# A hybrid recurrent step with expert retrieval: the loading of the tokens, the turning of the caches and the first retrieval groups in another order

## What is computed

```python
def layer(h, states, p, lead):
    mix, new = token_mixer(rmsnorm(h, p['ln1']), conv_buf, s_dn, shift_buf, s_rw, p, lead)
    h = h + mix
    f = peer_ffn(rmsnorm(h, p['ln2']).reshape(B * T, D), p['peer_wq'], p['peer_keys'], p['peer_u'], p['peer_v'])
    return h + f, new                      # then rmsnorm with ln_f

def peer_ffn(x, wq, keys, u_tab, v_tab):   # for every token t, head h: 16 of 16384 experts
    q = (xb @ wq).reshape(PEER_BLOCK, PEER_HEADS, 2, PEER_HALF)
    s = jnp.einsum('thpc,hpnc->thpn', q, keys)
    sv, si = lax.top_k(s, K)               # K = 16, in each half
    ...                                    # 16 best sums of the two halves, their expert numbers eidx
    gates = jax.nn.softmax(cv.astype(jnp.float32), -1)
    h = jax.nn.gelu(jnp.einsum('thkd,td->thk', u_tab[eidx], xb).astype(jnp.float32))
    return jnp.einsum('thk,thkd->td', (gates * h).astype(xb.dtype), v_tab[eidx])
```

## Time and profile before

| | us |
|---|---|
| median of three runs (1186.66 to 1190.22) | 1186.82 |
| the profiled execution | 1191.67 |
| its span, as the trace shows it | 1189.9 |
| PE busy in the span | 1003.9 |
| DVE busy | 712.4 |
| POOL busy (issuing gathers) | 518.2 |
| ACT busy | 271.3 |
| bytes moved by gathers, at 59% of 16 engines' span | 276.86 MB |

### The profile page before, as it was taken

One profiled execution on the slowest core, in us unless ns is written; L12 is line 12 of the kernel. 1 busy time (PEld: TensorE's weight loads), 2 busy tenths in 40 slices (PEclk: granted clock), 3 DMA queues, 4 the chain that ended last, 5 costly groups with the idle time before them and its releaser, 6 DMA issues.

```text
span 1189.9 us, 11394 instructions
## 1 busy us (share of the span) xinstructions
PE 1003.9 (84%) x3771; PEld 572.1 (48%) x3771; DVE 712.4 (60%) x1879; ACT 271.3 (23%) x644; POOL 518.2 (44%) x595
## 2 busy tenths in 40 slices
PE   4999898999998998979798777777777777777788
PEld 3887666879997653855343222222222222222221
DVE  1014673895264627696477657756766775676653
ACT  2127464014233011211112111111122111111111
POOL 3000010000000002575766777777777777777763
PEclk9999899998997999889899999999999999999999
DMA  8152020443216434989999999999999999999997
GB/s 278 38 211 77 0 73 11 100 130 112 72 72 226 145 104 145 405 340 360 403 390 371 403 410 409 410 409 409 409 409 409 409 409 410 408 408 409 391 374 279
DMA packets 119784, 334.26 MB, mean 281 GB/s; under 512 B 19087, under 2 KB 33266, under 8 KB 119462
## 3 DMA queue, kind: packets, MB, share of 16 engines
q0 software_dynamic: 76032, 276.86, 59.0%
q1 hardware_dynamic: 43694, 56.68, 14.8%
HBM read 326.99 MB, written 5.74 MB: 280 GB/s over the span
## 4 chain that ended last, share of the span: by engine, by line
PE 39%; DMA 25%; DVE 18%; POOL 10%; issue 5%; ACT 2%; SPq 1%; DVEq 0%; ACTq 0%; POOLq 0%
PE bank L1395 36%; DMA sb_all<-in_peer_u,idx 14%; DMA sb_all<-in_peer_v,idx 10%; POOL sb_all L585 10%; DVE sb_all L1120 3%; ACT sb_all L1791 2%; DVE sb_all L1098 1%; DVE sb_all L1096 1%; DVE sb_all L1100 1%; DVE sb_all L2274 1%; DVE sb_all L2271 1%; DMA sb_all<-in_w_in 1%; DVE key_i L1068 1%; DVE sb_all L1061 1%; DVE key_i L1062 1%
## 5 line engine op out<-in xcount | busy, mean ns | idle before, releaser
L1395 PE MATMUL bank<-sb_all 128*128 128x512 f32 (+15 forms) x3462 | 968.6, 433 | 150.7 <-DMA sb_all<-in_peer_v,idx 138.1
L1395 PEld LDWEIGHTS bank<-sb_all 128*128 128x128 f32 (+7 forms) x3462 | 540.8, 187 | 573.6 <-DMA sb_all<-in_peer_v,idx 311.6
L1120 DVE CUSTOM_DVE_ANT_0 sb_all<-sb_all,bank 128x1024 f32<-128x1024 f32 x264 | 314.2, 1220 | 173.3 <-DMA sb_all<-in_peer_u,idx 172.8
L585 POOL DMA_INDIRECT sb_all<-in_peer_u,idx x264 | 251.5, 953 | 229.7 <-DVE idx L1104 103.3
L585 POOL DMA_INDIRECT sb_all<-in_peer_v,idx x264 | 250.9, 950 | 84.9 <-issue 68.6
L1791 ACT ACTIVATE sb_all<-sb_all 128x128 f32<-128x128 f32 (+11 forms) x367 | 145.1, 421 | 532.7 <-PE bank L1395 382.3
L1791 ACT ACTIVATE sb_all<-bank 128x264 f32<-128x264 f32 (+15 forms) x183 | 82.9, 468 | 362.8 <-PE bank L1395 312.1
L620 POOL IOTA sb_all<- 128x54 f32 x1 | 0.2, 183 | 166.5 <-PE bank L1395 166.5
L1385 POOL MEMSET sb_all<- 128x3456 f32 x1 | 3.0, 2984 | 142.8 <-DVE sb_all L2185 142.8
L2068 DVE SCALAR_TENSOR_TENSOR sb_all<-sb_all 128x288 f32<-128x288 f32 x14 | 6.1, 513 | 60.7 <-ACT sb_all L1791 60.7
L1791 ACT ACT_TABLE_LOAD x23 | 29.5, 1283 | 13.8 <-POOL sb_all L1364 9.5
(11 more groups left out here) (230 smaller groups left out, 435.1 us busy)
## 6 DMA issues: line engine op xcount, KB each, us to landing
sb_all<-in_w_in SPq DMA_DIRECT2D x9, 2048.0 KB, 7.7
sb_all<-in_peer_wq SPq DMA_DIRECT2D x4, 2048.0 KB, 16.0
sb_all<-in_w_in SPq DMA_DIRECT2D x5, 1024.0 KB, 5.2
sb_all<-in_peer_u,idx POOLq DMA_INDIRECT x264, 10.3
sb_all<-in_peer_v,idx POOLq DMA_INDIRECT x264, 10.4
out<-sb_all SPq DMA_DIRECT2D x8, 512.0 KB, 4.8
sb_all<-in_w_out SPq DMA_DIRECT2D x2, 2048.0 KB, 8.3
sb_all<-in_x_prompt SPq DMA_DIRECT2D x4, 512.0 KB
```

What stands on the lines that cost most here:

```text
L585: pool.indirect_dma_start(ring[at % 8], None, table[0], bass.IndirectOffsetOnAxis(ap=idx[:, c:c + 1], axis=0)).then_inc(landed[at % 8], 16)
L1120: v.tensor_tensor_reduce(uring[i % 8], uring[i % 8], x, 1.0, 0.0, ALU.mult, ALU.add, hdot[:, u % 2, j:j + 1]).then_inc(u_free, 1)
L1395: return nc.tensor.matmul(out, lhsT, rhs, start=start, stop=stop, **kw)
```

## The change

Beginning: six of the parameter loads are issued by ACT's own queue, the other five stay on SP; the caches and the six small loads go behind the weights `r`. POOL makes `ident` and the first `eps` column first and counts `consts` for them, then the other constants (the table `level` has only its two used planes filled). ACT takes a root of `eps` first, then for each tile, when it has landed, the square and the root. The caches are turned on PE between the projections of `r` and `kr`, and copied out by ACT after the first four output tiles.

Retrieval: on DVE the rest of the residual and the norms of tiles 1 and 2 come before any dot, then eight dots of unit 0, the second selection, the other eight. On ACT the Tanh of unit 0 comes before the copy of the fourth query tile, the softmax exponent of unit 1 behind the scores, and the Tanh of units 1, 2 and 3 at slots 8, 8 and 10 in place of 12. On POOL four v rows are gathered behind u row 15.

```diff
@@ retrieval, POOL: pool_peer
+            AHEAD = 4
             for i in range(NSLOT + LAG):
...
                     gather(pool, uring, u_in, peer_u, i, i)
-                if i >= LAG:
+                if i == PT - 1:
+                    for n in range(AHEAD):
+                        gather(pool, vring, v_in, peer_v, V_ORDER[n], n)
+                if i >= LAG + AHEAD:
@@ retrieval, ACT: act_rest
             softmax_exp(0)
-            softmax_exp(1)
             queried(0, slice(128, NX), 4, lambda q: psv(2 + q % 2, 128, NX - 128))
             scored(0, 1)
             scored(0, 2)
-            for q in range(4):
+            for q in range(3):
                 queried_all(1, q)
             gelu(0)
+            queried_all(1, 3)
             pair_scored(1)
+            softmax_exp(1)
+            GELU_AT = {0: 8, 1: 8, 2: 10}
...
-                    if j == 12 and u + 1 < UNITS:
+                    if j == GELU_AT.get(u, 12) and u + 1 < UNITS:
                         gelu(u + 1)
@@ retrieval, DVE: vec_rest
             topk(0)
             residual(3)
-            topk(1)
-            norm(1, 128)
             residual(4)
             residual(5)
-            dots(0, 0, 2)
+            norm(1, 128)
             norm(2, NS)
-            dots(0, 2, PT)
+            dots(0, 0, PT // 2)
+            topk(1)
+            dots(0, PT // 2, PT)
             weights(0)
@@ beginning, SP
-            for name, n in PAR:
+            emit_parameters(sp, PAR[6:])
...
-            sp.dma_start(cconv[0:24, :], cache_dn_conv[0].rearrange("b j n -> (b j) n")).then_inc(small_in, 16)
-            sp.dma_start(cshift[0:8, :], cache_rw_shift[0, :, 0]).then_inc(small_in, 16)
...
                 sp.dma_start(dst, src).then_inc(w_landed[slot], 16)
                 if n == 0:
+                    sp.dma_start(cconv[0:24, :], cache_dn_conv[0].rearrange("b j n -> (b j) n")).then_inc(small_in, 16)
+                    sp.dma_start(cshift[0:8, :], cache_rw_shift[0, :, 0]).then_inc(small_in, 16)
                     sp.dma_start(lora[0:64, :], rw_w2[0]).then_inc(small_in, 16)
@@ beginning, POOL
+            step(nc.gpsimd.memset(ident, 0.0))
+            step(nc.gpsimd.memset(eps[:, 0:1], 1e-6))
+            step.sync()
+            nc.gpsimd.affine_select(out=ident, in_=ident, pattern=[[-1, 128]], compare_op=ALU.not_equal, fill=1.0,
+                                    base=0, channel_multiplier=1).then_inc(consts, 1)
...
-            for l in range(LEVELS + 1):
+            for l in (LEVELS - 1, LEVELS):
@@ beginning, PE
-                    pe.wait_ge(small_in, 16 * 8)
...
             pe.wait_ge(xT_done, 8)
-            for name in ("r", "kr", "vr", "wag"):
+            pe.wait_ge(consts, 2)
+            project("r")
+            pe.wait_ge(small_in, 16 * 8)
+            for f in range(12):
+                nc.tensor.transpose(psv(7, 128, 24, at=24 * f), cconv[0:24, f * 128:(f + 1) * 128],
+                                    ident[0:24, 0:24])
...
+            for name in ("kr", "vr", "wag"):
                 project(name)
@@ beginning, ACT
-            act.wait_ge(x_in, 64)
+            emit_parameters(act, PAR[:6])
             act.wait_ge(consts, 1)
+            step(fn(eps[:, 3:4], eps[:, 0:1], ACT.Sqrt))
             for i, n in enumerate(TILE_ROWS):
+                act.wait_ge(x_in[i].sem, x_in[i].at(16 if i < 2 else 32))
                 step(fn(xs[0:n, i, :], xtok[0:n, i, :], ACT.Square, accum_out=ss[0:n, i:i + 1]))
-            for i, n in enumerate(TILE_ROWS):
-                step.sync(2 - i)
+                step.sync()
                 fn(rs[0:n, i:i + 1], ss[0:n, i:i + 1], ACT.Sqrt, scale=1.0 / D,
                    bias=eps[0:n, 0:1]).then_inc(rs_ready, 1)
```

More of the change, by code:

```diff
@@ L259, in hybrid_step @@
         w_landed = [sem(f"w_landed{i}") for i in range(3)]
-        x_in = sem("x_in")
+        x0_in = Signal(sem("x0_in"), 0)
+        x1_in, rows_in = series(sem("x1_rows_in"), 16, 32)
+        x2_in, keys_in = series(sem("x2_keys_in"), 32, 16)
+        x_in = [x0_in, x1_in, x2_in]
         small_in = sem("small_in")
@@ L1234, in hybrid_step, with emit_parameters @@
         block = ctx.enter_context(nc.Block())
-        @block.sync
-        def _(sp):
-            sp.dma_start(xtok[:, 0, :], x_prompt[0, 0:128]).then_inc(x_in, 16)
-            sp.dma_start(xtok[:, 1, :], x_prompt[0, 128:256]).then_inc(x_in, 16)
-            sp.dma_start(xtok[0:NS, 2, :], x_sample[:, 0]).then_inc(x_in, 16)
-            sp.dma_start(xtok[NS:NS + META, 2, :], meta_tokens).then_inc(x_in, 16)
+        def emit_parameters(eng, rows):
             srcs = {"ln1": ln1, "mu": rw_mu, "w0": rw_w0, "a0": rw_a0, "k_k": rw_k_k, "k_a": rw_k_a, "gn_w": rw_gn_w,
                     "gn_b": rw_gn_b, "dn_norm": dn_norm_w}
-            for name, n in PAR:
+            for name, n in rows:
                 if name == "conv":
@@ L1251, in _ @@
                     src = srcs[name][0].rearrange("(f p) -> f p", p=128)
[L1252 to L1254 removed]
+                eng.dma_start(parrow[PAR_AT[name]:PAR_AT[name] + n, :], src).then_inc(par_in, 16)
+        @block.sync
+        def _(sp):
+            sp.dma_start(xtok[:, 0, :], x_prompt[0, 0:128]).then_inc(x0_in.sem, 16)
+            sp.dma_start(xtok[:, 1, :], x_prompt[0, 128:256]).then_inc(x1_in.sem, 16)
+            sp.dma_start(xtok[0:NS, 2, :], x_sample[:, 0]).then_inc(x2_in.sem, 16)
+            sp.dma_start(xtok[NS:NS + META, 2, :], meta_tokens).then_inc(x2_in.sem, 16)
+            emit_parameters(sp, PAR[6:])
             for n, (name, src, slot, width, use) in enumerate(items):
@@ L1322, in _ @@
             step = Steps(pool, pool_step)
-            for t, v in ((ones, 1.0), (ident, 0.0), (halves, 0.0), (incl, 1.0), (strict, 1.0),
-                         (level, 0.0), (reset, 1.0), (ba, 0.0), (prw[:, :, 0:1 + PAD], 0.0),
+            step(nc.gpsimd.memset(ident, 0.0))
[3 more added lines that the diff above has]
+                                    base=0, channel_multiplier=1).then_inc(consts, 1)
+            for t, v in ((ones, 1.0), (halves, 0.0), (incl, 1.0), (strict, 1.0),
+                         (level[:, LEVELS - 1:, :], 0.0), (reset, 1.0), (ba, 0.0), (prw[:, :, 0:1 + PAD], 0.0),
                          (pre[:, :, 0:3 + PAD], 0.0), (xnT[:, :, 0:PAD], 0.0)):
                 step(nc.gpsimd.memset(t, v))
-            step(nc.gpsimd.memset(eps[:, 0:1], 1e-6))
             step(nc.gpsimd.memset(eps[:, 1:2], DK * 1e-6))
             step(nc.gpsimd.memset(eps[:, 2:3], 64e-5))
-            step.sync()
-            step(nc.gpsimd.affine_select(out=ident, in_=ident, pattern=[[-1, 128]], compare_op=ALU.not_equal,
-                                         fill=1.0, base=0, channel_multiplier=1))
             step.sync()
@@ L1410, in _ @@
                                         ident[0:PAR_ROWS, 0:PAR_ROWS]).then_inc(par_t.sem, 1)
-                    pe.wait_ge(small_in, 16 * 8)
-                    for f in range(12):
-                        nc.tensor.transpose(psv(7, 128, 24, at=24 * f), cconv[0:24, f * 128:(f + 1) * 128],
-                                            ident[0:24, 0:24])
-                    for f in range(14):
-                        ins = nc.tensor.transpose(psv(7, 128, 8, at=288 + 8 * f), cshift[0:8, f * 128:(f + 1) * 128],
-                                                  ident[0:8, 0:8])
-                    ins.then_inc(cache_t.sem, 1)
             tile = [0]
@@ L1435, in _ @@
             pe.wait_ge(xT_done, 8)
-            for name in ("r", "kr", "vr", "wag"):
+            pe.wait_ge(consts, 2)
[4 more added lines that the diff above has]
+                                    ident[0:24, 0:24])
+            for f in range(14):
+                ins = nc.tensor.transpose(psv(7, 128, 8, at=288 + 8 * f), cshift[0:8, f * 128:(f + 1) * 128],
+                                          ident[0:8, 0:8])
+            ins.then_inc(cache_t.sem, 1)
+            for name in ("kr", "vr", "wag"):
                 project(name)
@@ L1814, in evacuate @@
                     tile[0] += 1
-            evacuate([prw[:, f, 1 + PAD:1 + NC] for f in range(14)])
+            act.wait_ge(consts, 2)
+            evacuate([prw[:, f, 1 + PAD:1 + NC] for f in range(4)])
+            act.wait_ge(cache_t.sem, cache_t.at(1))
+            fn(cconvT.rearrange("p f c -> p (f c)"), psv(7, 128, 288)).then_inc(cache_ready.sem, 1)
+            fn(cshiftT.rearrange("p f c -> p (f c)"), psv(7, 128, 112, at=288)).then_inc(cache_ready.sem, 1)
+            evacuate([prw[:, f, 1 + PAD:1 + NC] for f in range(4, 14)])
             act.wait_ge(ba_ready.sem, ba_ready.at(1))
```

23 lines of the change are left out of this document (9 added, 14 removed).

## The result

| | before | after |
|---|---|---|
| median, us (four runs each, side by side) | 1188.37 (1186.66 to 1190.22) | 1174.11 (1173.01 to 1175.55) |
| ratio of after to before, 95% interval | | 0.988 (0.9858 to 0.9903) |
| the profiled execution, us | 1191.67 | 1174.37 |
| first gather in it, us | 461.92 | 447.87 |
| from there to the end, us | 729.75 | 726.50 |

The kernel became 14.3 us faster (11.5 to 16.9), where 18.6 were forecast. The time lies in the forecast's whole range (1162.0 to 1178.5), 5.9 us above the forecast and just past the 1174 up to which its own mechanism was to reach; its two halves fit less well. By the two profiles the beginning and what runs on from it gave 14.05 us to the first gather, against 9.1 forecast, and the retrieval 3.25 us, against 9.5.

What follows compares the result with a forecast made beforehand. A wait chain through PE bounds it up to the first gathers, then the DMA engines at 409 GB/s. Gains of 9.1 + 4.5 + 1.0 + 4.0 = 18.6 us take 1186.82 to 1168.2, range 1162.0 to 1178.5.

Steps and rivals of the forecast that it cites:

- rival (a): Retrieval: the queue still runs dry, late selections starving POOL at u rows 16 and 32; 1176 us, chance 0.18.
- Up to the first gathers nothing is tied to a fixed time: From 25.54 us to the first gathers: if the projections start earlier by some amount, so does everything up to there.
- The beginning, 9.1 us: Start of the kernel: `r` begins 12.0 us sooner, less 2.9 for the moved cache transposes; bounds 6.6 to 11.1.
- ACT's table load: Beginning, on ACT: a change of tables costs 1.30 us; by the skill page's 2.66 the sum would be 17.2.
- The hole at row 24, 4.5 of 5.2 us: Retrieval, unit 0, 500 to 520 us: sooner Tanh and fuller queue win 3.0 to 5.2 us, taken 4.5.
- the margin at row 32: Retrieval: queued rows last to 526.5; u row 32 waits for the third selection until 524.0, covering from 528.
- 540 to 580, 1.0 of 4.0 us: Retrieval: unit 1's Tanh stall goes, but most of the loss is the sixteen sample-row copies; 0 to 4.0, taken 1.0.
- Units 2 and 3, 4.0 of 4.5: Retrieval, 600 to 660 us: Tanh ahead of the score copies and a fuller queue win 0 to 4.5, taken 4.0.
- Time is lost only where the queue runs dry: DMA-bound retrieval: rates below 409 GB/s were read as a dry queue, losing 5.2, 4.0 and 4.5 us.
- (b): Beginning: gives only 2 us, as ACT's loads or `r` land late; 1175 us, chance 0.08.
- (c): Retrieval, unit 0: an early Tanh blocks ACT, delaying diagonals for PE, then v rows and POOL; slower, 1191 us, chance 0.03.
- (d): No change: a dry queue at 497 or 526 or a hidden transfer swallows the gain; 1186.8 us, chance 0.05.

Runs made afterwards that it cites:

- Tanhs only: The kernel after with POOL's and DVE's order of the retrieval put back, beginning and ACT's order still changed: 1172.12 us, ratio to before 0.9867.

## Why the prediction was right, and where not

That the time fell within the range owes something to luck: the beginning with its clock came out above its sum, the retrieval at half of its own (4.8 of 9.5), and the range was made wide enough for rival (a). The forecast also started from 1186.82; from the 1188.37 measured side by side it would have been 1169.8. And 1174 as the upper end of its own range does not follow from its sum, whose lower bound of 9.6 us gives 1177.2.

1. *Up to the first gathers nothing is tied to a fixed time.* Held: 11.77 us at `r`, 10.15 at the first tile of `kr`, 14.05 at the first gather.

2. *The beginning, 9.1 us.* Right at the place that it was worked out for, 9.0 on the mean of ten at the first tile of `kr`; in the medians 11.2 (8.4 to 13.9), just past the upper bound of 11.1. Two terms were off and made up for each other. The start of `r` was forecast at 13.5 and came at 13.77 to 15.03: the step "they are in by 10.6 to 12.6 and don't decide, with a margin of 1 us" failed: in all ten the landing of the weights ended PE's wait, 0.9 to 2.2 us behind DVE (12.85 us). In after's own stretches 3.40 MB had passed by 11.6 us (4.2 us at 197 GB/s, 7.4 at 347), enough for the tokens and `r` together (3.29), so the rates were right. But `r` was not in: some of these bytes must have been those of loads issued behind it, from 4.64 us on, and the rest came slowly (which load each byte belonged to, no row shows):

```profile
0.00:4.20 4.20, 0.00 (x0) 0.00 (x0) 0.00 (x0) 0.90 (x1) 3.17 (x23) 1.00 0.55 197
4.20:11.60 7.40, 4.30 (x23) 4.00 (x23) 4.54 (x11) 4.84 (x12) 4.40 (x23) 1.00 1.02 347
11.60:13.70 2.10, 0.39 (x5) 0.28 (x4) 1.25 (x6) 0.00 (x0) 0.00 (x0) 1.00 1.00 167
```

Here a load's end was not its bytes by a rate while others were issued behind it. The caches cost 1.74 in place of 2.87 us: I carried over the duration of the old place, where the engines moved 388 GB/s beside it; what made them slower there was not tested, the clock was 1.00 in both. What the granted clock adds between `kr` and the first gather, up to 4.2 us between the ten profiles, no term held.

3. *ACT's table load.* The first root started at 4.60, 1.30 us after the start of a load of 1.28 us, so 1.30 for a change of tables holds again. The Trainium skill (ScalarE: Activation LUTs, "What ACT_TABLE_LOAD costs") has 2.66 us for it; no drain of 1.38 us shows here either.

4. *The hole at row 24, 4.5 of 5.2 us.* It closed as forecast, and DVE's first dot of unit 1 came as forecast (490.36 + 14.05 = 504.4 in the times of before, 505.0 forecast). But A as a whole fell by 2.5 to 3.1 us only. The step that failed is the margin at row 32: forecast for 524.0, it came at 511.94 + 14.05 = 526.0, mostly because the eight dots ahead of the third selection took 10.65 us (490.36 to 501.01) in place of 9.13: DVE waited in between for rows to land (0.43 us ahead of the second dot, 0.37 ahead of the third). Rival (a) was right that a hole moves to row 32, wrong about row 16, where the rate held (408 GB/s to 512.87), and its 1176 has too little for the rest. The attribution was wrong too: I took the four v rows and the late selection for part of the cure. The runs show that the sooner Tanh closes row 24 without either (*Tanhs only*, A 1.1), that the v rows are needed only for the row 16 which the late selection leaves dry, and that it is they that open row 32. What they issue ahead of row 16 is missing behind row 24: the sum counted twelve rows there, and the margin was 1 to 2 us.

5. *540 to 580, 1.0 of 4.0 us.* Right in mechanism, the copies; but nothing was won there: B was 3.9 and stayed at 4.0 to 4.5.

6. *Units 2 and 3, 4.0 of 4.5.* Right: 4.6 became 0.6. The term that was missing is D, 2.3 to 2.8 us given back from 648 us on, where the forecast had the rate stay at 409.

7. *The reading behind 4 to 6.* "Time is lost only where the queue runs dry" is wrong. The earlier trace rows already had a share of 1.02 at 368 GB/s beside one of 0.83 at 303; only the second is a dry queue.

Of the rivals, (a) came in part, at row 32. (b), (c) and (d) did not come: PE had `r` 11.8 us sooner, the time is 14.3 us shorter, and no stretch shows the rate falling for want of a diagonal in unit 0.

## What to carry to other kernels

Where the DMA engines bound a stage, read the DMA share beside the rate: a low share asks for sooner issue, a full share with a low rate asks which small transfers are in the way, and these are better not sent at all. When a change moves several things at once towards one stall, cost each alone: here one moved instruction of 0.2 us on ACT closed the hole, and four gathers sent ahead opened the next one. When a part is put back, see what else now waits in front of it: one exponent, put back with the Tanhs, held ACT for 11.2 us. Of a profiled execution, compare stretches from an event of its own (here the first gather), since what lies before it differs by some us from run to run.
